# Opening's sums of squares moved into the loop over x, and the first two blocks of four down stages interleaved

## The chip, the cores and the metric

One core of one Trainium2 chip runs the whole program. The metric is the device time of one execution in microseconds (us), and a shorter time is better. Each kernel is executed several times; the median is given. A profile of one further execution gives the times of single instructions.

## The reference

A two-layer trunk works on 512 prompt tokens and 8 x 16 sample tokens, 640 columns in all, with a residual stream `x` of width 1024. Each layer does

```python
x = x + 0.5 * swiglu(rmsnorm(x, norm_g[i, 0]), ffn_w_gu[i, 0], ffn_w_d[i, 0])
x = x + mixer_i(rmsnorm(x, norm_g[i, 1]))      # even: gated DeltaNet and mLSTM heads; odd: gated short convolution
x = x + 0.5 * swiglu(rmsnorm(x, norm_g[i, 2]), ffn_w_gu[i, 1], ffn_w_d[i, 1])
x = x + (p[i] @ w_ple[i]) * sigmoid(rmsnorm(x, norm_g[i, 3]) @ w_ple_gate[i])

def rmsnorm(x, g):
    return x * rsqrt(mean(x * x) + EPS) * g
def swiglu(x, w_gu, w_d):
    a, b = split(x @ w_gu, 2)
    return (silu(a) * b) @ w_d
```

and a last rmsnorm follows. Everything is fp32. The hidden width of a feed-forward block is 2816.

## The kernel before

**Layout.** The residual stream lies transposed in SBUF: `x[:, q, :]` holds features 128q to 128q+127 on the partitions and all 640 tokens along the row, for q = 0 to 7. Every product is made of three matmuls per tile: high parts (`xh`, `hh`, `whi`) and low parts (`xl`, `hl`, `wlo`) of both operands, without the product of the low parts. A weight block of `kt` tiles of 128 x 128 times 640 tokens takes 6 matmuls of 320 columns per tile (`mm`, L898): high x high (L913) and high x low (L914) for both halves of the tokens, then low x high (L917). So a block of 8 tiles is 48 matmuls, and one of 6 tiles 36.

**The engines.** PE (TensorE) multiplies. SP issues the weight loads into `raw`, which has four places. ACT (ScalarE) casts a block of raw weights to `whi` (`prep(n)`, L1595, cast in L1607), POOL (GpSimd) subtracts to get `wlo` (L861), and DVE (VectorE) does most of what comes out of PSUM. `whi` and `wlo` are a ring of three places for blocks: `prep(n)` waits until the block that last had that place is done on PE. Each engine runs its own instruction list strictly in order, written out by hand; semaphores join them. `job_done` counts finished PE jobs; `lo_ready` counts finished `wlo`; `h_ready` counts finished hidden tiles; `xg_ready` counts finished tiles of the normed stream's low part; `slot_free` guards the four PSUM slots.

**The opening.** PE transposes x tile by tile (L982), and between these it runs step q of the first two weight blocks g0 and g0+1 (gate and up of the first hidden tile). Per tile, ACT copies x out of PSUM (L1787) and scales it to `xh` (L1650); DVE copies the sample columns (`x_rest`, L2723) and makes `xl` (`x_low`, L2269). DVE also has sums of x tiles to make for a fast form of the paired products that comes later, `tau_row`: for each of four i one `tau_back` (L2235) and four operations (`tau_sums`, L2228 to L2231), of which i = 0, 1, 2 lie in the loop. After the loop DVE copies three states out of PSUM (L2754 to L2756). Only then come the eight squares on ACT (L1813, alternately into `qcopy` and `stt`) and the eight additions on DVE (`square_sum`, L2278 and L2280, into `sumsq`), in lock step. PE runs block g0+2 meanwhile; then `norm_job` (L972, matmul in L968) needs the finished `sumsq`. Its root (ACT, L1732) and the reciprocal `r` (DVE, L2366) are needed by the gates. `plain_start` on DVE (called in the first feed-forward stage) does `tau_rest` 0 and 1 (the low part `tau_lo`, L2244), the reciprocal, the copied gate (L2822), `tau_sums_alone(3)`, the copied hidden tile, the gate of block 2, and so on down to the first pair's `wlo` (`pair_low`, L2197). Then come the paired products (L928 to L930). The first pair needs `pair_low(0, 0)` at its start and, 24 matmuls later, `pair_low(0, 1)` and all of `tau_lo`.

**The down stages.** Each of the four feed-forward blocks has its 22 hidden tiles in three parts, of 8, 8 and 6 tiles. After each part a down stage of eight blocks n0 to n0+7 follows, with kt = 8, 8 and 6. In it PE waits at each k of block n0 for hidden tile k. DVE does for block o: `ut = ps * r` (L2181), `x = ut * -0.5 + x` (L2919), and in the third part, the last, `produce`: the square's sum and `x_low` (L2280, L2269). ACT does for block o: `prep(n0+o+2)`, and in the last part the square (L1659) and `xh` (L1650) as soon as x is new. In the second feed-forward block of a layer the input p is transposed (`pT`, two jobs) behind block n0+1, and DVE copies and splits it (L2941, L2943) behind block n0+1's own work. What follows the four last parts is the even mixer's input projection, the first ple stage, the odd mixer's input projection and the second ple stage. The first block of each needs `xl` of all eight tiles.

These four last down stages are called A, B, C and D below, in order of time. The place in the ring that block n0+2 or n0+3 gets depends on how many blocks follow until the next pairs: in A and C, n0+2 has a place of its own and n0+3 takes the place of n0+1; in B, n0+2 takes the place of n0; in D, n0+3 takes that of n0.

## Time and profile before

| what | us |
|---|---|
| median of three runs | 2714.54 (2713.57 to 2715.55) |
| the profiled execution's own time | 2713.01 |
| its span, first to last instruction | 2711.3 |
| PE busy in it | 2652.8 (98%) |
| DVE busy | 1863.9 (69%) |
| ACT busy | 1075.4 (40%) |
| POOL busy | 524.6 (19%) |
| PE waiting for the sum of squares (L968) | 5.1 |
| PE waiting for hidden tiles' low parts (L2793) | 4.0 + 2.9 |

The mean granted TensorE clock of the execution is 0.991 of full speed. All times in the trace count from the first instruction. Timeline rows read: start, duration, engine, line, operation, output<-inputs, shapes, count, and in brackets the idle time ahead of it with what ended it. Matmul durations overlap, so the time of a piece of work on PE is read from start to start.

### The profile page before, as it was taken

How to read it: one execution, taken by the hardware profiler on the slowest of the kernel's cores; microseconds unless marked ns; L12 is line 12 of the kernel's file. 1: busy time of each engine (PE TensorE's matmuls, PEld its weight loads, DVE VectorE, ACT ScalarE, POOL GpSimd, SP SyncE). 2: the span in 40 equal slices, each digit the busy share in tenths (PEclk: the TensorE clock that was granted, in tenths of full speed). 3: DMA queues.
4: the chain of work that ended last, by engine and by line, in shares of the span. 5: the costliest groups of instructions: out<-in, count | busy, mean ns of one | idle time of the engine just before them, and what ended most of it. 6: DMA issues, size and time to landing. Idle time of an engine off the chain costs nothing.

```text
span 2711.3 us, 43605 instructions
## 1 busy us (share of the span) xinstructions
PE 2652.8 (98%) x18155; PEld 2613.9 (96%) x18155; DVE 1863.9 (69%) x2188; ACT 1075.4 (40%) x1565; POOL 524.6 (19%) x249
## 2 busy tenths in 40 slices
PE   7999999999999999999999999999999999999998
PEld 7999999999998799999999999999999999999998
DVE  7748386988667768576577874847666786584756
ACT  5525254233222645344244552524411254252545
POOL 1030303232010030201113302030333311102041
PEclk9999999999999999999999999999999999999999
DMA  4323223232003122323232232232222223232231
GB/s 122 86 71 89 83 75 90 55 81 55 17 9 86 54 72 78 94 78 94 63 88 70 71 101 71 78 94 75 83 78 79 63 78 94 63 95 65 82 101 50
DMA packets 401180, 205.57 MB, mean 76 GB/s; under 512 B 15586, under 2 KB 398971, under 8 KB 400984
## 3 DMA queue, kind: packets, MB, share of 16 engines
q1 hardware_dynamic: 400778, 202.70, 26.4%
q8 instruction: 144, 2.36, 0.4%
q14 instruction: 52, 0.43, 0.1%
q10 hardware_dynamic: 206, 0.08, 0.0%
HBM read 195.14 MB, written 7.60 MB: 75 GB/s over the span
## 4 chain that ended last, share of the span: by engine, by line
PE 54%; DVE 9%; ACT 2%; issue 1%; POOL 0%; DVEq 0%; ACTq 0%
PE ps L928 9%; PE ps L930 9%; PE ps L929 9%; PE ps L913 9%; PE ps L917 8%; PE ps L914 8%; DVE ut L2181 1%; DVE x L2919 1%; DVE sumsq L2280 1%; DVE r L2366 1%; DVE hf L2787 1%; DVE x L3105 0%; DVE wlo L2197 0%; DVE hl L2269 0%; PE ps L1198 0%
## 5 line engine op out<-in xcount | busy, mean ns | idle before, releaser
L861 POOL TENSOR_TENSOR wlo<-raw,whi 128x1024 fp32r<-128x1024 f32 (+2 forms) x212 | 513.1, 2423 | 2147.0 <-ACT whi L1607 2146.6
L913 PE MATMUL ps<-xh,whi 128*128 128x320 f32 x1520 | 464.0, 313 | 12.1 <-POOL wlo L861 4.7
L914 PE MATMUL ps<-xl,whi 128*128 128x320 f32 x1520 | 458.4, 309 | 0.0
L913 PE MATMUL ps<-hh,whi 128*128 128x320 f32 x1440 | 437.6, 312 | 5.1 <-DVE hl L2793 2.9
L914 PE MATMUL ps<-hl,whi 128*128 128x320 f32 x1440 | 434.8, 310 | 0.0
L928 PE MATMUL ps<-tau_hi,whi 128*128 128x320 f32 x1296 | 401.3, 310 | 2.1 <-DVE wlo L2197 2.0
L929 PE MATMUL ps<-tau_lo,whi 128*128 128x320 f32 x1296 | 400.5, 309 | 0.0
L930 PE MATMUL ps<-tau_hi,wlo 128*128 128x320 f32 x1296 | 400.5, 309 | 0.0
L1607 ACT CAST whi<-raw 128x1024 fp32r<-128x1024 f32 (+2 forms) x214 | 206.7, 967 | 395.0 <-PE ps L917 355.6
L917 PE MATMUL ps<-xh,wlo 128*128 128x320 f32 x1520 | 347.1, 310 | 0.0
L917 PE MATMUL ps<-hh,wlo 128*128 128x320 f32 x1440 | 329.1, 310 | 0.0
L2181 DVE TENSOR_TENSOR ut<-ps,r 128x640 f32<-128x640 f32 x112 | 92.4, 825 | 328.0 <-PE ps L917 327.0
L913 PEld LDWEIGHTS ps<-xh,whi 128*128 128x128 f32 x1520 | 286.3, 188 | 18.5 <-issue 11.0
L914 PEld LDWEIGHTS ps<-xl,whi 128*128 128x128 f32 x1520 | 286.3, 188 | 0.9 <-issue 0.2
L1618 ACT CAST whi<-raw 128x512 fp32r<-128x512 f32 (+1 forms) x243 | 185.0, 766 | 246.9 <-PE ps L930 125.6
L913 PEld LDWEIGHTS ps<-hh,whi 128*128 128x128 f32 x1440 | 271.4, 189 | 8.1 <-DVE hl L2793 4.5
L914 PEld LDWEIGHTS ps<-hl,whi 128*128 128x128 f32 x1440 | 271.3, 188 | 0.4
L917 PEld LDWEIGHTS ps<-xh,wlo 128*128 128x128 f32 x1520 | 254.7, 188 | 0.0
L928 PEld LDWEIGHTS ps<-tau_hi,whi 128*128 128x128 f32 x1296 | 243.2, 188 | 4.5 <-issue 3.9
L929 PEld LDWEIGHTS ps<-tau_lo,whi 128*128 128x128 f32 x1296 | 243.3, 188 | 0.0
L930 PEld LDWEIGHTS ps<-tau_hi,wlo 128*128 128x128 f32 x1296 | 243.3, 188 | 0.0
L917 PEld LDWEIGHTS ps<-hh,wlo 128*128 128x128 f32 x1440 | 241.4, 188 | 0.0
(433 smaller groups left out, 4829.4 us busy)
## 6 DMA issues: line engine op xcount, KB each, us to landing
raw<-in_ffn_w_gu SPq DMA_DIRECT2D x324, 256.0 KB, 3.9
raw<-in_ffn_w_d SPq DMA_DIRECT2D x64, 512.0 KB, 4.0
raw<-in_w_in_even SPq DMA_DIRECT2D x32, 512.0 KB, 4.1
raw<-in_ffn_w_d SPq DMA_DIRECT2D x32, 384.0 KB, 3.6
raw<-in_w_in_odd SPq DMA_DIRECT2D x24, 512.0 KB, 3.7
raw<-in_w_ple_gate SPq DMA_DIRECT2D x16, 512.0 KB, 3.9
raw<-in_ffn_w_gu SPq DMA_DIRECT2D x14, 512.0 KB, 4.6
raw<-in_w_out_even SPq DMA_DIRECT2D x8, 512.0 KB, 4.0
```

Of the source, the lines that this page charges most:

```text
L861: pool.tensor_tensor(ring(wlo, n), raw[:, slot, 0:kt, :], ring(whi, n).bitcast(fp32), ALU.subtract).then_inc(lo_ready, 1)
L913: pe.matmul(ps[j % 4][:, c, 0:HT], wh[:, k], hi[:, k, cs], start=(k == 0), stop=False)
L914: pe.matmul(ps[j % 4][:, c, 0:HT], wh[:, k], lo[:, k, cs], start=False, stop=False)
L917: last = pe.matmul(ps[j % 4][:, c, 0:HT], wl[:, k], hi[:, k, cs], start=False, stop=(k == kt - 1))
L928: pe.matmul(out, whi[:, w], hi(i), start=(start and i == 0), stop=False, skip_group_check=True)
L929: pe.matmul(out, whi[:, w], lo(i), start=False, stop=False, skip_group_check=True)
L930: last = pe.matmul(out, wlo[:, w], hi(i), start=False, stop=(i == KH - 1), skip_group_check=True)
L1607: act.copy(ring(whi, n), raw[:, raw_pos["block", n], 0:kt, :]).then_inc(hi_ready, 1)
L1618: act.copy(group_ring(whi, g), group_raw(p, g)).then_inc(pair_hi, 1)
L2181: o1(dve.tensor_tensor(out, a, b, ALU.mult))
L2280: own(dve.tensor_tensor(sumsq[:], sumsq[:], src, ALU.add).then_inc(sm, 1), sm)
L2366: o1(dve.reciprocal(r[:], r[:]))
```

## The change

On PE, in down stages with fewer than 8 tiles per block (the four last parts), the first two blocks run together: five k steps of n0, five of n0+1, then the sixth of n0 and the sixth of n0+1. Blocks n0+2 to n0+7 stay as they were.

On ACT, the square of tile q-2 stands inside the loop over x, behind `xh` of tile q, for q = 2 to 7; the squares of tiles 6 and 7 stand behind the loop, ahead of the copies of g0 and g0+1 and of `prep(3)`.

On DVE, the addition of tile q-3 stands inside the loop from q = 3, with `tau_back(0)` at q = 5. The tau sums 0, 1 and 2 leave the loop and stand behind the last addition, ahead of the reciprocal. In `plain_start`, `tau_rest(t, 1)` moves behind the copied gate and `tau_sums_alone(3)` behind the gate of block 2.

```diff
@@ PE
                 elif kind == "down":
                     if s.get("split"):
                         first_blocks(s)
+                    hidden = (h_ready, s["hbase"])
+                    both = s["kt"] < KD
+                    if both:
+                        for part in ((0, s["kt"] - 1), (s["kt"] - 1, s["kt"])):
+                            for o in range(2):
+                                mm(s["n0"] + o, *s["hid"], first=hidden, part=part)
                     for o in range(2 if s.get("split") else 0, KD):
-                        mm(s["n0"] + o, *s["hid"], first=(h_ready, s["hbase"]) if o == 0 else None)
+                        if not both or o > 1:
+                            mm(s["n0"] + o, *s["hid"], first=hidden if o == 0 else None)
@@ ACT
+                    def square(q):
+                        if q >= 2:
+
+                            act.wait_ge(sq_added, q - 1)
+                        act.activation([qcopy, stt][q % 2][:], x[:, q, :], ACT.Square).then_inc(sq_ready, 1)
+
                     for q, j in enumerate(s["x"]):
...
                         x_high(0, q, 0)
                         if q == 0:
                             prep(1)
+                        if q >= 2:
+                            square(q - 2)
                     prep(2)
...
-                    for q in range(KD):
-                        if q >= 2:
-
-                            act.wait_ge(sq_added, q - 1)
-                        act.activation([qcopy, stt][q % 2][:], x[:, q, :], ACT.Square).then_inc(sq_ready, 1)
-                        if q == 3:
-                            first_out(0, gt)
-                            prep(3)
-                        if q == 5:
-                            first_out(1, ut)
+                    square(KD - 2)
+                    square(KD - 1)
+                    first_out(0, gt)
+                    prep(3)
+                    first_out(1, ut)
@@ DVE
                         x_low(0, q, 0)
-                        i = q // 2 - 1
-                        if i >= 0 and q % 2 == 0:
-                            tau_back(i)
-                        elif i >= 0:
-                            tau_sums(0, i, 0)
+                        if q >= 3:
+                            square_sum(0, q - 3)
+                            dve.sem_inc(sq_added, 1)
+                        if q == 5:
+                            tau_back(0)
...
-                    for q in range(KD):
+                    for q in range(KD - 3, KD):
                         square_sum(0, q)
                         dve.sem_inc(sq_added, 1)
+                    tau_sums(0, 0, 0)
+                    tau_sums_alone(1)
+                    tau_sums_alone(2)
@@ DVE, plain_start
                         tau_rest(t, 0)
-                        tau_rest(t, 1)
                         norm_recip(s)
                         copied_gate()
-                        tau_sums_alone(3)
+                        tau_rest(t, 1)
                         copied_hidden()
                         plain_gate(1)
+                        tau_sums_alone(3)
                         tau_rest(t, 2)
```

On PE at the start of down stage A, before: n0 accumulates in `ps3`, n0+1 in `ps0`. The first row is the end of step k = 4 of n0, the next five are its last step.

```order
2523 L917 MATMUL ps3<-hh_56,wlo_54 128x320 x2
2524 L913 MATMUL ps3<-hh_56,whi_53 128x320 [waits h_ready]
2525 L914 MATMUL ps3<-hl_57,whi_53 128x320
2526 L913 MATMUL ps3<-hh_56,whi_53 128x320
2527 L914 MATMUL ps3<-hl_57,whi_53 128x320
2528 L917 MATMUL ps3<-hh_56,wlo_54 128x320 x2
2529 L913 MATMUL ps0<-hh_56,whi_53 128x320 [waits lo_ready,slot_free0]
```

The same rows of the changed kernel:

```order
2523 L917 MATMUL ps3<-hh_56,wlo_54 128x320 x2
2524 L913 MATMUL ps0<-hh_56,whi_53 128x320 [waits h_ready,lo_ready,slot_free0]
2525 L914 MATMUL ps0<-hl_57,whi_53 128x320
2526 L913 MATMUL ps0<-hh_56,whi_53 128x320
2527 L914 MATMUL ps0<-hl_57,whi_53 128x320
2528 L917 MATMUL ps0<-hh_56,wlo_54 128x320 x2
2529 L913 MATMUL ps0<-hh_56,whi_53 128x320 [waits h_ready]
```

The last step of n0 now stands 30 matmuls later, behind five steps of n0+1, and n0 and n0+1 end within six matmuls of each other. The same happens in stages B, C and D.

On DVE in the opening, before: from the last addition of the squares to the copied hidden tile.

```order
47 L2280 TENSOR_TENSOR sumsq<-sumsq,stt 128x640 [waits dve_own,sq_ready]
48 L2244 TENSOR_TENSOR tau_lo<-tau_row,tau_hi 128x1280 [waits sumsq_done,tau_high]
49 L2244 TENSOR_TENSOR tau_lo<-tau_row,tau_hi 128x1280 [waits tau_high,tau_low]
50 L2366 RECIPROCAL r<-r 128x640 [waits root_ready,tau_low]
51 L2822 TENSOR_TENSOR gt<-gt,r 128x640 [waits slot_free2,dve_own]
52 L2235 TENSOR_SCALAR xg_back<-x,vec_109 128x320 [waits gate_in]
```

The same stretch of the changed kernel:

```order
33 L2290 TENSOR_TENSOR sumsq<-sumsq,stt 128x640 [waits dve_own,sq_ready]
34 L2238 SCALAR_TENSOR_TENSOR tau_row<-x,vec_109,xg_back 128x320 [waits sumsq_done,back_ready]
35 L2239 SCALAR_TENSOR_TENSOR tau_row<-x,vec_109,xg_back 128x320 [waits dve_own]
...
47 L2241 SCALAR_TENSOR_TENSOR tau_row<-x,vneg,tau_row 128x320 [waits dve_own]
48 L2254 TENSOR_TENSOR tau_lo<-tau_row,tau_hi 128x1280 [waits tau_high,tau_ready]
49 L2376 RECIPROCAL r<-r 128x640 [waits root_ready,tau_low]
50 L2835 TENSOR_TENSOR gt<-gt,r 128x640 [waits slot_free2,dve_own]
51 L2254 TENSOR_TENSOR tau_lo<-tau_row,tau_hi 128x1280 [waits tau_high,gate_in]
```

The last addition moves from place 47 to place 33 of DVE's list, but the reciprocal only from 50 to 49: fourteen tau operations stand between them now, and one `tau_lo` moved behind the gate. DVE's list up to the first pair holds the same instructions in both.

## Rows read from the trace of the kernel before

**Rows 1.** Waits of PE: engine, line waited for: us in total, times, longest.

```profile
PE ps L968 <- DVE sumsq L2280: 5.1, 2, 4.9
PE ps L913 <- DVE xl L2793: 4.0, 6, 1.5
PE ps L913 <- DVE hl L2793: 2.9, 6, 0.8
```

**Rows 2.** Timeline of PE, opening: g0+2's last matmuls, the norm's, first tau product.

```profile
40.77 0.46 PE L917 MATMUL ps<-xh,wlo 128*128 128x320 f32 x2
46.09 2.50 PE L968 MATMUL ps<-sumsq,one 128*128 128x320 f32 x4 [4.87 <-DVE sumsq L2280]
...
74.10 0.31 PE L928 MATMUL ps<-tau_hi,whi 128*128 128x320 f32 x1
```

**Rows 3.** Busy time by stretches: us, PE, PEld, DVE, ACT, POOL (x), PEclk, DMA share, GB/s.

```profile
46.09:50.80 4.71, 4.71 (x14) 3.92 (x15) 3.39 (x3) 4.51 (x5) 2.54 (x1) 0.50 0.32 88
1416.45:1448.20 31.75, 31.75 (x219) 31.75 (x218) 24.76 (x31) 11.53 (x17) 11.13 (x6) 1.00 0.17 50
```

**Rows 4.** Timeline of DVE, opening.

```profile
30.14 2.61 DVE L2228 SCALAR_TENSOR_TENSOR tau_row<-x,vec,xg_back 128x320 f32<-128x320 f32 x1
32.78 0.55 DVE L2229 SCALAR_TENSOR_TENSOR tau_row<-x,vec,xg_back 128x320 f32<-128x320 f32 x1
...
40.66 2.46 DVE L2280 TENSOR_TENSOR sumsq<-sumsq,qcopy 128x640 f32<-128x640 f32 x1 [1.09 <-ACT qcopy L1813]
46.19 3.02 DVE L2244 TENSOR_TENSOR tau_lo<-tau_row,tau_hi 128x1280 fp32r<-128x1280 f32 x2
50.40 4.15 DVE L2366 RECIPROCAL r<-r 128x640 f32<-128x640 f32 x1 [1.19 <-ACT r L1732]
...
66.86 1.22 DVE L2197 TENSOR_TENSOR wlo<-raw,whi 128x1024 fp32r<-128x1024 f32 x1
...
70.42 1.76 DVE L2197 TENSOR_TENSOR wlo<-wsum,whi 128x1536 fp32r<-128x1536 f32 x1
```

**Rows 5.** Timeline of POOL, opening: the low part of block g0+2.

```profile
30.02 2.37 POOL L861 TENSOR_TENSOR wlo<-raw,whi 128x1024 fp32r<-128x1024 f32 x1 [25.35 <-ACT whi L1607]
```

**Rows 6.** Timelines of DVE, ACT, POOL and PE, down stage A and its end.

```profile
427.05 0.83 DVE L2919 SCALAR_TENSOR_TENSOR x<-ut,x 128x640 f32<-128x640 f32 x1
...
432.33 2.46 DVE L2919 SCALAR_TENSOR_TENSOR x<-ut,x 128x640 f32<-128x640 f32 x1
...
467.80 0.89 DVE L2269 SCALAR_TENSOR_TENSOR xl<-x,vec,xh 128x640 fp32r<-128x640 f32 x1
...
431.35 0.84 ACT L1607 CAST whi<-raw 128x768 fp32r<-128x768 f32 x1 [1.97 <-PE ps L917]
...
432.26 1.85 POOL L861 TENSOR_TENSOR wlo<-raw,whi 128x768 fp32r<-128x768 f32 x1 [5.77 <-ACT whi L1607]
...
468.93 0.31 PE L913 MATMUL ps<-xh,whi 128*128 128x320 f32 x1
```

**Rows 7.** Timelines of ACT, DVE, POOL and PE, down stage B and the ple stage's start.

```profile
1410.42 0.84 ACT L1607 CAST whi<-raw 128x768 fp32r<-128x768 f32 x1 [2.22 <-PE ps L917]
...
1411.40 2.47 DVE L2919 SCALAR_TENSOR_TENSOR x<-ut,x 128x640 f32<-128x640 f32 x1
...
1411.33 1.86 POOL L861 TENSOR_TENSOR wlo<-raw,whi 128x768 fp32r<-128x768 f32 x1 [7.76 <-ACT whi L1607]
...
1429.92 2.05 POOL L861 TENSOR_TENSOR wlo<-raw,whi 128x768 fp32r<-128x768 f32 x1 [6.84 <-ACT whi L1607]
...
1432.38 0.31 PE L913 MATMUL ps<-hh,whi 128*128 128x320 f32 x1
...
1452.82 0.38 PE L913 MATMUL ps<-xh,whi 128*128 128x320 f32 x1 [0.32 <-issue]
```

**Rows 8.** Timelines of POOL and PE, down stage D and the second ple stage's start.

```profile
2600.64 2.06 POOL L861 TENSOR_TENSOR wlo<-raw,whi 128x768 fp32r<-128x768 f32 x1 [6.84 <-ACT whi L1607]
...
2636.37 0.38 PE L913 MATMUL ps<-hh,whi 128*128 128x320 f32 x1 [0.99 <-issue]
```

## The prediction, made before the changed kernel was run

> **What bounds the kernel now.** I read three views: PE's waits, for where it loses time; the timelines of all engines around those waits, for what a removed wait runs into; and the busy time by stretches, for the clock and for PE's pace. PE is busy for nearly the whole span, so an edit can win only a wait on PE or a stretch of low clock, and lose only by a new one. Two waits are aimed at. One is for the sum of squares, 4.87 us at once: the last matmul of block g0+2 begins at 40.92, the norm's at 46.09 [rows 1, 2]. Behind it PE works until 50.80 at a granted clock of 0.50, so at 1.2 GHz, and 0.50 x 4.71 = 2.4 us of work are lost with it [rows 3]. The other is for the low part of the sixth hidden tile in down stages A to D: 0.84 us each in A to C, where the wait for `hl` is at most 0.8, and 1.5 in D [rows 1]; with the pipeline's restart about 1.0, 1.0, 1.0 and 1.7, 4.7 us in all. PE's pace at full clock: the six blocks n0+2 to n0+7 of stage B take 31.75 us [rows 3], 5.29 a block of 36 matmuls, 0.88 a k step, 0.147 a matmul.
>
> **The rule that decides both parts.** When a DVE operation with both inputs in SBUF starts while POOL subtracts, it ends after POOL does: the tau sum at 30.14 took 2.61 us and ended at 32.75, POOL ran from 30.02 to 32.39; its next neighbour takes 0.55 [rows 4, 5]. The new x of n0+1 in stage A began at 432.33, took 2.46 instead of 0.83 and ended at 434.79, 0.68 after POOL's 434.11 [rows 6]. Operations that read PSUM aren't held up.
>
> **Part 1, down stages.** Five steps of n0+1 are put ahead of n0's last: 30 x 0.147 = 4.4 us. The hidden tile is late by 1.0 (D: 1.7), so this wait on PE goes whole. But n0 now ends at 66 matmuls from the stage's start instead of 36 and the wait: 9.69 instead of 6.39, so 3.3 us later (D: 2.6). On n0's end hangs a chain: DVE's `ut` and new x, ACT's square and `xh`, ACT's cast of a later block (in order behind them), POOL's `wlo`, DVE's next new x, held until POOL ends, and round again. One round is 0.03 + 1.37 on ACT, 0.90 for the cast, 2.04 on POOL, 0.68 on DVE: 5.0 us, and 5.6 for blocks of 8 tiles. PE needs 5.29. So the chain runs nearly at PE's pace and a delay at its head isn't made good in six rounds; its two ends are the next blocks' `wlo` and the eighth `xl`.
> Stage B. The cast of n0+2 waits for n0's end (ring place), at 1410.42; then POOL from 1411.33 to 1413.19 and the new x until 1413.87 [rows 7]. All of it moves 3.3 later. POOL ends block n0+2 at 1416.5, where PE would want it at 1415.4: 1.2 us of waiting, which eats the 1.0 won. Three blocks on, `wlo` of n0+5 ended at 1431.97 and PE began that block at about 1432.3, so 0.35 us of slack [rows 7]; with 3.3 it ends at 1435.3, and PE, whose own time for it would be 1432.5, waits 2.7 us. The ple stage's first gate began right behind a wait for POOL, at 1452.82 [rows 7]: no slack, so it moves the full 3.3. Stage B: +3.3 us.
> Stage A. n0+2 has a place of its own. The cast of n0+3 waited for n0+1's end and began at 431.35 [rows 6]. n0's new x ends at 427.88 + 3.3 = 431.18; with 1.40 for square and `xh` the cast begins at 432.58, 1.23 later, and so do POOL and every round behind. PE at n0+3: POOL ends at 435.35, PE wants it at 435.28, a wait of 0.2. The eighth `xl` ended at 468.69 and PE began with it at 468.93, 0.24 of slack [rows 6]; now 469.92, and with 0.1 for the restart PE is 1.1 later than before: a new wait of 1.9 us replaces one of 1.0. What follows is a DVE and ACT chain from the norm on and moves with it. Stage A: +1.1. Stage C has the same ring places and the same rows 1494.9 us later, with the same slack: +1.1.
> Stage D. n0 ends 2.6 later; n0+1's new x, which POOL didn't hold up before, now meets POOL and gets 2.2 later, and the chain with it. `wlo` of n0+5 ended at 2602.70 [rows 8], now 2604.9, PE wants it at 2602.5: a wait of 2.4. Then the ple stage's eight short blocks go through ACT's casts and copies, and the first gate waits behind POOL at 2636.37 [rows 8]. +2.1, and at least +0.8 if that piece has slack that I don't see.
> Sum: 3.3 + 1.1 + 1.1 + 2.1 = +7.6 us. Bounds: if none of the chain's delay reaches PE, -4.7; if all chains move by 3.3, +13. I take 7.6, since in each stage the row at the end has a slack of 0.35 us or less.
> The Trainium skill, "Perfetto Trace Analysis", Optimization Strategy, says to work on what blocks the matmul engine when it idles; by that alone the four waits go and the part is worth -4.7 us. No run here shows that yet, and the rows above speak against it.
>
> **Part 2, the opening.** The squares and additions of tiles 0 to 4 fill DVE's time in the loop where tau sums stood. A walk with the rows' durations: PE's two short waits for `xl` in the loop (1.05 together with restarts) go, g0+2 ends at 39.7, `sumsq` is done at 35.4, so PE doesn't wait for it, and the norm ends at 40.5. Then g0+3 to g0+5 take 3 x 7.05 and PE wants the first pair at 61.7, where before it began near 70.6. That would be 8.9 us.
> But DVE must have done the same list first. From the first addition until `wlo` at 70.42 ends (72.18), DVE before has two waits, 1.09 and 1.19, and two holds by POOL, 2.06 and 1.63 [rows 4]. Now: sum done 35.4; tau sums 0 to 2, 7.9 us, of which the second operation meets POOL's block g0+3 (35.8 to 38.3) and loses 2.0: 45.4; ACT's cast of g0+4 comes behind the high part of tau 1, so POOL runs from 45.0 to 47.6 and holds the first `tau_lo`: 49.0 instead of 47.0. The root is ready by 47.1. The reciprocal starts at 49.0, 1.4 earlier than its 50.40 [rows 4]. Behind it stands all that stood there, 21.8 us until the end at 72.18, and one `tau_lo` of 1.5 more (two take 3.02) [rows 4]: 72.3. The first pair's `wlo` (66.86 + 1.2 [rows 4]) comes at 68.1 as before. So PE waits 6.2 us ahead of the first pair instead of 4.9 ahead of the norm. Its third product, at 74.10 [rows 2], can start at 72.3 at full clock: 1.8 won. After a wait of this length the clock was low until 4.7 us behind the restart [rows 3]; then the two first products take 5.9 instead of 3.5 us and it starts at 74.1: nothing won. I take -0.7, between these; -1.8 and +0.9 (low clock for longer) are the bounds.
> Who meets POOL first decides 2 us of this. The Trainium skill, "SBUF — State Buffer", Who interferes with whom, says that whoever issues first gets the shared port pair for the whole instruction. By it, if the cast of g0+4 comes a few tenths later, `tau_lo` is first and the reciprocal starts at 47.1: 1.9 us more won here. The trace agrees with the rule: in rows 4 and 5 POOL is first and DVE waits.
> The rest (the copies of g0 and g0+1 and `prep(3)`, 3 to 4 us earlier on ACT; the raw loads of the first pair, which wait for POOL) has cover of several us and costs nothing.
>
> **Sum.** 7.6 - 0.7 = +6.9 us. The profiled execution took 2713.01 us, 1.53 under the median; 2719.9 there, 2721.4 against the median of 2714.54.
>
> **Rivals.**
> 1. The chain has slack that I don't see, as meant by the edit: the down stages win 4.7 and the opening 0.7: 2709.1. For it: DVE is busy only 69% and has waits in every round. Against: the waits are for ACT and POOL in the same chain.
> 2. The opening gives its 8.9 us, since DVE or POOL are quicker there than I walked, and the down stages cost 7.6: 2713.2. It needs DVE to save 7 us in a list that is the same.
> 3. Both: 2714.5 - 8.9 - 4.7 = 2700.9, faster.
> 4. The new waits, 6.2 us in the opening, 2.7 in B, 2.4 in D, each bring a stretch of low clock. Each costs up to 1.7 us; in B and D part of it lies in the slack of the rounds behind. Slower: 2723 to 2726, say 2724.5. It counts from the point where a wait of 2.4 to 2.7 us is followed by clock 0.50; the wait of 1.5 in D [rows 1] wasn't.
>
> **How the numbers follow.** My forecast, 2721.4 with 2718.5 to 2724, gets 0.62; rival 1 0.10, rival 2 0.12, rival 3 0.04, rival 4 0.12. The range from 2712.5 to 2725.5 leaves out rivals 1 and 3 and the tail of 4, 0.18. A difference under 0.2%, 5.4 us, can't be told from none here. Slower by more is above 2720.0: 0.62 less 0.08 for its lower end, and 0.12 of rival 4: 0.66. Within: 0.08, rival 2 and half of rival 1: 0.25. Faster by more: 0.09.
>
> **What would show it.** In the profile after: PE no longer waits at L968; it waits some 6 us for DVE's `wlo` ahead of L928 near 62 us, and pair 0's tau products begin near 73. In stages A to D no wait for L2793; instead `wlo` (L861) waits of 1.2 and 2.7 us in B and of 2.4 in D, and `xl` (L2269) waits of 1.9 at the first block behind A and C. New x of n0 3.3 us later against the stage's start, of n0+7 1.2 (A, C), 3.3 (B), 2.2 (D). It is wrong if the last new x isn't later, or if DVE reaches the reciprocal before 46.

## The result, and the profile after

| | before | after |
|---|---|---|
| median of 20 runs each, us | 2713.35 (2707.69 to 2721.57) | 2722.64 (2716.47 to 2730.21) |
| profiled execution, us | 2713.01 | 2728.32 |
| its span, us | 2711.3 | 2726.6 |
| ratio | | 1.0036 [1.0025, 1.0046] |

The changed kernel is slower: +9.8 us by the ratio (6.8 to 12.5), +9.3 by the medians. The prediction had +6.9 and 2721.4.

PE's waits in the changed kernel (engine, line waited for: us in total, times, longest), against [rows 1]:

```profile
PE ps L913 <- POOL wlo L861: 11.7, 16, 2.7
...
PE ps L928 <- DVE wlo L2207: 6.6, 10, 3.7
PE ps L913 <- DVE xl L2279: 3.7, 2, 2.1
PE ps L913 <- DVEq L2195: 2.9, 1, 2.9
...
PE ps L913 <- DVE hl L2279: 1.7, 1, 1.7
...
PE ps L913 <- DVE hl L2806: 1.3, 4, 0.3
```

The wait of 4.9 us for `sumsq` is gone, and of the waits for `hl` and `xl` of the hidden tiles (now L2806) only eight of at most 0.3 us are left. In their place stand waits for POOL's `wlo`, up to 2.7 us, for the eighth `xl` ahead of the next stage, 1.67 behind A and 1.68 behind C (in the row with `hl` of L2279, since the low parts of the next stage's operand lie in that buffer there), and in the opening 2.9 for a slot of PSUM and 3.7 for the first pair's `wlo`. The 2.1 us in the row for `xl` of L2279 is no new wait: it lies at 12.60 us, in the loop over x, where the kernel before waits 2.35.

**Opening.** Timelines of PE, DVE and POOL in the changed kernel:

```profile
39.66 0.70 PE L968 MATMUL ps<-sumsq,one 128*128 128x320 f32 x2
...
57.90 0.41 PE L913 MATMUL ps<-xh,whi 128*128 128x320 f32 x1 [2.86 <-DVEq L2195]
...
68.89 0.61 PE L928 MATMUL ps<-xh,whi 128*128 128x320 f32 x1 [3.69 <-DVE wlo L2207]
...
35.60 2.68 DVE L2238 SCALAR_TENSOR_TENSOR tau_row<-x,vec,xg_back 128x320 f32<-128x320 f32 x1 [0.57 <-DVE sumsq L2290]
...
45.18 2.79 DVE L2241 SCALAR_TENSOR_TENSOR tau_row<-x,vneg,tau_row 128x320 f32<-128x320 f32 x1
48.00 1.49 DVE L2254 TENSOR_TENSOR tau_lo<-tau_row,tau_hi 128x1280 fp32r<-128x1280 f32 x1
49.52 4.15 DVE L2376 RECIPROCAL r<-r 128x640 f32<-128x640 f32 x1
...
35.52 2.41 POOL L861 TENSOR_TENSOR wlo<-raw,whi 128x1024 fp32r<-128x1024 f32 x1 [3.11 <-ACT whi L1614]
45.21 2.41 POOL L861 TENSOR_TENSOR wlo<-raw,whi 128x1024 fp32r<-128x1024 f32 x1 [7.28 <-ACT whi L1614]
48.54 3.22 POOL L861 TENSOR_TENSOR wlo<-raw,whi 128x1024 fp32r<-128x1024 f32 x1 [0.92 <-ACT whi L1614]
```

PE reaches the norm 6.4 us earlier (46.09 before [rows 2]) and doesn't wait for it. But the reciprocal starts at 49.52, where it started at 50.40 [rows 4], since POOL holds two DVE operations ahead of it, 2.68 and 2.79 us where the neighbours take 0.55. PE then waits 2.9 and 3.7 us.

**Stage B.** Timelines of ACT, POOL, DVE and PE in the changed kernel, the answers to [rows 7]. This stage begins 7.60 us later than in the kernel before (ACT's `hh` of the sixth hidden tile, 1407.47 and 1415.07), so 7.60 is to be taken off:

```profile
1421.31 0.84 ACT L1614 CAST whi<-raw 128x768 fp32r<-128x768 f32 x1 [5.51 <-PE ps L917]
...
1422.23 1.80 POOL L861 TENSOR_TENSOR wlo<-raw,whi 128x768 fp32r<-128x768 f32 x1 [11.06 <-ACT whi L1614]
1422.29 2.42 DVE L2932 SCALAR_TENSOR_TENSOR x<-ut,x 128x640 f32<-128x640 f32 x1
...
1424.18 0.38 PE L913 MATMUL ps<-hh,whi 128*128 128x320 f32 x1 [0.99 <-POOL wlo L861]
...
1440.78 2.00 POOL L861 TENSOR_TENSOR wlo<-raw,whi 128x768 fp32r<-128x768 f32 x1 [6.84 <-ACT whi L1614]
...
1442.92 0.60 PE L913 MATMUL ps<-hh,whi 128*128 128x320 f32 x1 [2.67 <-POOL wlo L861]
...
1460.54 1.05 ACT L1614 CAST whi<-raw 128x1024 fp32r<-128x1024 f32 x1 [0.83 <-PE ps L917]
...
1461.67 2.96 POOL L861 TENSOR_TENSOR wlo<-raw,whi 128x1024 fp32r<-128x1024 f32 x1 [0.53 <-ACT whi L1614]
```

The cast of n0+2 comes 3.29 us later against the stage (1413.71 for 1410.42), n0's new x ends 3.24 later, POOL's low part of n0+5 ends at 1435.18 instead of 1431.97, 3.21 later: the whole delay is still there after three rounds. PE waits 1.0 and 2.7 us for it. Behind the second wait the clock is low (0.52, so mostly at 1.2 GHz); busy time of that stretch, with the granted clock as the third last number:

```profile
1442.92:1446.32 3.40, 3.40 (x13) 3.40 (x14) 2.46 (x4) 2.18 (x3) 0.58 (x1) 0.52 0.13 39
```

The ple block's cast, which waits for PE, comes 4.1 us later (1448.84 before), its low part on POOL ends 4.3 later, and so does the first gate: 1464.73 for 1452.82 [rows 7], less 7.60: +4.31.

**Stages A and D.** DVE and PE behind stage A; PE in stage D:

```profile
469.76 0.89 DVE L2279 SCALAR_TENSOR_TENSOR xl<-x,vec,xh 128x640 fp32r<-128x640 f32 x1
...
470.70 0.42 PE L913 MATMUL ps<-xh,whi 128*128 128x320 f32 x1 [1.67 <-DVE xl L2279]
...
2618.20 0.39 PE L913 MATMUL ps<-xh,whi 128*128 128x320 f32 x1 [2.30 <-POOL wlo L861]
```

The eighth `xl` ends 0.05 us before PE takes it, as the slack of 0.24 in [rows 6] let expect, and PE waits 1.67 us there. In D the wait for n0+5 is 2.3 us.

### The profile page after: what moved, and what is told of

Same layout as the page of the kernel before. It is cut to its first block, busy times and chain, and to the rows that moved or that the text cites. A ratio compares the mean times of both kernels' runs of the same rounds, so it can differ in the third digit from the quotient of the medians.

```text
span 2726.6 us, 43607 instructions
## 1 busy us (share of the span) xinstructions
PE 2661.7 (98%) x18155; PEld 2621.2 (96%) x18155; DVE 1862.6 (68%) x2188; ACT 1074.2 (39%) x1565; POOL 524.8 (19%) x249
## 4 chain that ended last, share of the span: by engine, by line
PE 80%; DVE 16%; ACT 2%; issue 1%; POOL 0%; DMA 0%; DVEq 0%; SPq 0%; ACTq 0%
PE ps L928 12%; PE ps L930 12%; PE ps L929 12%; PE ps L913 11%; PE ps L917 11%; PE ps L914 11%; PE ps L1057 3%; DVE x L2932 2%; PE ps L1083 2%; DVE ut L2191 1%; DVE sumsq L2290 1%; DVE ct L2987 1%; DVE r L2376 1%; DVE ct L2984 1%; PE ps L1051 1%
```

## The experiments

**How they are read.** The medians move by whole steps from one execution to the next: the same changed kernel took 2716 to 2730 us. So each kernel's profile is also cut into stretches that are compared one by one, from a fixed matmul to a fixed matmul: A from the last pair's first tau product ahead of the stage to the norm behind it (before: 385.98 to 469.81), B 1333.30 to 1459.93, and C, D and what lies between 1530.12 to 2643.48. The stretch from 469.81 to 1033.68 stands apart. Differences to the kernel before, in us; the last two columns are the length of that stretch, and where PE starts pair 0's tau products (74.10 before):

| kernel | A | B | C to D | 469.81 to 1033.68 | tau products |
|---|---|---|---|---|---|
| before | 0 | 0 | 0 | 563.87 | 74.10 |
| changed | +1.17 | +4.32 | +3.43 | 569.60 | 74.79 |
| changed, once more | +1.13 | +4.35 | +3.38 | 568.69 | 73.58 |
| down stages alone | +1.18 | +4.36 | +3.26 | 562.70 | 74.17 |
| stage B alone | 0.0 | +4.36 | 0.0 | 563.92 | 74.59 |
| opening alone | 0.0 | 0.0 | +0.12 | 565.54 | 74.46 |
| opening, fewer additions | 0.0 | 0.0 | -0.06 | 562.09 | 72.73 |
| one step ahead | -0.88 | -0.06 | -1.38 | 569.29 | 74.55 |
| one step, once more | -0.89 | -0.06 | -1.35 | 566.11 | 74.70 |
| three steps ahead | -0.57 | +1.44 | -0.19 | 569.29 | 74.83 |
| root first | 0.0 | 0.0 | +0.16 | 559.87 | 72.68 |
| root first, tau low part late | 0.0 | 0.0 | +0.15 | 563.18 | 70.60 |
| root first, one step | -0.89 | -0.03 | -1.19 | 563.80 | 72.03 |
| all three | -0.88 | -0.04 | -1.16 | 571.04 | 69.93 |

**The down stages alone** (e_down), and **the opening alone** (e_open): the two halves of the change, one each. The diff shows the first; the second is the change without it.

```diff
-for o in range(2 if s.get("split") else 0, KD):
-    mm(s["n0"] + o, *s["hid"], first=(h_ready, s["hbase"]) if o == 0 else None)
+hidden = (h_ready, s["hbase"])
+both = s["kt"] < KD
+if both:
+    for part in ((0, s["kt"] - 1), (s["kt"] - 1, s["kt"])):
+        for o in range(2):
+            mm(s["n0"] + o, *s["hid"], first=hidden, part=part)
...
```

> The kernel before with the interleaved first two blocks in the four last down stages, opening as before. Theory (delay at the head of a chain of DVE, ACT and POOL): the stretches of the trace from n0's start to the next stage move by +1.2, +4.3, +1.2 and +2.1 us as in the profile after, +8.8 in all, and the time is 1.0030 to 1.0035 of before; no wait for the hidden tile's low part is left in the four stages. Rival (the cost sits elsewhere: in the profile after, the mixer's core between 656 and 1038 us took 5.8 us more than before): then the core is 5 to 6 us longer here as well, and the four stages together cost under 5.

Measured: 2720.29 us, ratio 1.0035 [1.0024, 1.0046].

> The kernel before with the new order in the opening alone. Theory (DVE's list up to the first pair is the floor): no wait at the norm, but waits of about 3 us at block g0+5 and 3.7 us ahead of the first pair; the down stage that began at 138.8 in before's trace begins 0.7 later; the time is within 0.1% of before. Rival (the opening wins once the down stages don't hide it): 4 to 9 us faster, 0.997 to 0.9985. The core between the first projection and the second feed-forward block takes what it took before, within what single profiles scatter.

Measured: 2713.36 us, ratio 0.9991 [0.9976, 1.0005]. So the down stages carry all of the loss, 8.8 us by the stretches, and the opening nothing that a median shows. Pair 0's tau products begin between 74.10 and 74.83 us in six profiles with the old opening and between 73.58 and 74.79 in three with the new one; the means are 0.2 us apart. Most of the spread within one kernel is the clock: in the changed kernel PE starts the first pair at 68.89 and the 5.90 us until the tau products go at a granted clock of 0.57, in its second profile it starts at 69.36 and needs 4.22 us at 1.00. There the low clock came earlier, behind the wait of 2.85 us for the slot (0.54 over the 3.40 us from 58.37), and it only shortened the wait ahead of the first pair, 2.16 us instead of 3.69. The stretch from the first pair to the tau products, in the first profile and in the second:

```profile
68.89:74.79 5.90, 5.90 (x25) 5.90 (x26) 5.58 (x7) 2.71 (x5) 0.00 (x0) 0.57 0.00 0
...
69.36:73.58 4.22, 3.76 (x24) 3.50 (x24) 4.04 (x5) 2.75 (x6) 0.00 (x0) 1.00 0.00 0
```

**Stage B alone** (e_down_b).

```diff
-both = s["kt"] < KD
+both = s["kt"] < KD and "pT" in s and s["layer"] == 0
```

> Interleaved only in the down stage ahead of the first ple stage (B). Theory: B's stretch is 3.3 to 4.3 us longer (4.3 if the wait of 2.7 us ahead of block n0+5 brings a stretch of low clock, 3.3 if not), all other stages as before. Rival (the four stages' costs depend on each other, or the low clock alone makes B's cost): B costs under 2 us by itself.

Measured: 2717.42 us in one run. Stage B costs the same 4.36 us with the others undone, so its cost doesn't come from them.

**One step ahead instead of five** (e_one_step), **three** (e_three_steps). The last step of n0 waits for the sixth hidden tile; one or three steps of n0+1 are put ahead of it (the diff is the one with one step; with three, 3 stands for both 1s of n + 1).

```diff
...
+mm(n, *s["hid"], first=hidden, part=(0, kt - 1))
+mm(n + 1, *s["hid"], first=hidden, part=(0, 1))
+mm(n, *s["hid"], first=hidden, part=(kt - 1, kt))
+mm(n + 1, *s["hid"], part=(1, kt))
...
```

> Down stages A to D with one k step of n0+1 (6 matmuls, 0.88 us) ahead of n0's last instead of all five; opening as in the kernel before. Theory (a chain through ACT's cast, POOL and DVE starts at n0's end and has almost no slack): the step fills 0.88 of the wait of about 1.0 for the hidden tile, and n0 ends 0.1 to 0.2 us EARLIER than before, so no chain is late. Stages A and C win 0.9 each, since there the ring place is n0+1's, whose end moves 0.9 forward too; B, whose ring place is n0's, wins 0.1 to 0.5; D 0 to 0.9, since its hidden tile is 1.7 late. Sum -2 to -3 us, ratio 0.9990 to 0.9993, and no wait for wlo over 1 us. Rival (any step of n0+1 ahead of n0 brings the cost, by the ring places or by two blocks that end close together): +1 us or more, with wlo waits of 2 us in B and D as in the changed kernel.

Measured: 2716.21 us, ratio 1.0011 [1.0002, 1.0020], on its face the rival's result. By the stretches the down stages do what the theory says, A -0.88, B -0.06, C -0.87 and D -0.45, -2.3 in all; PE's wait for n0+5 in B is 0.45 us at 1437.06, and only one wait for `wlo` in D, 1.17 us at 2629.86, is above the 1 us that the theory allowed. The loss lies elsewhere (569.29 us for 563.87 in this profile), in the stretch behind 469 us that has none of these stages in it; it comes back below.

> As the last, with three k steps of n0+1 ahead (18 matmuls, 2.64 us). n0 ends 1.6 us later than before in A to C, 0.9 in D. Theory, with a threshold in each stage: A and C: the cast of n0+3 is bound by n0's new x only from 2.07 us of delay on, so nothing of the loss and the whole gain, -1.0 each; B: the chain moves the full 1.6 less its slack of 0.35, +1.3, and its wait for wlo of n0+5 shrinks from 2.7 to about 1.3 with no low clock behind it; D +0.4. Sum -0.3 us. Rival (the cost grows evenly with the steps put ahead, between one and five): +3.4 us.

Measured: 2719.12 us, ratio 1.0016 [1.0004, 1.0027]; stretches A -0.57, B +1.44, C -0.58, D +0.41, in all +0.7, where the theory had -0.3 and a cost that grows evenly +3.4. In A and C the cost doesn't grow evenly: against the one step, a delay of n0 of 1.6 us costs 0.3 there, and one of 3.3 costs 2.1. A line through the two begins at a delay of about 1.3 us, an estimate; the 2.07 that was expected is too high. In B 1.6 us of delay cost 1.5. The wait for n0+5 in B is 2.2 us, not 1.3 as written: PE comes 0.9 earlier and POOL 1.6 later, and the text had only counted the second. The clock stays at 1.00 behind it:

```profile
1439.17:1442.57 3.40, 3.40 (x23) 3.40 (x24) 2.46 (x4) 2.18 (x3) 0.57 (x1) 1.00 0.13 39
```

**What DVE has to do ahead of the reciprocal** (e_few_sums): the opening alone, with the additions of tiles 1 to 6 to the sum of squares left out (the sum then holds two of eight tiles, and the time is that of a kernel which does less).

```diff
+def few_sum(q):
+    if q in (0, KD - 1):
+        square_sum(0, q)
+    else:
+        dve.wait_ge(sq_ready, q + 1)
+    dve.sem_inc(sq_added, 1)
```

> The new order in the opening alone, with the additions of the squares of tiles 1 to 6 left out (the waits and signals around them stay), so the opening's norm is computed from two tiles of eight. It takes some 5 us of DVE work away ahead of the reciprocal. Theory (DVE's list is the floor): the reciprocal starts 3 to 5 us earlier than the 49.5 of the changed kernel, and the first pair's tau products 3 to 6 us earlier than 74.8. Rival (PE's, ACT's or POOL's own chain or the PSUM slot of block g0+5 is the floor): under 1.5 us.

Measured: 2709.75 us in one run. Counted from the transposes of the conv state (30.68 in the opening alone, 29.56 here, since the two executions are 1.1 us apart by then), the reciprocal starts at 18.67 instead of 20.19, 1.5 us earlier, and the first pair at 38.04 instead of 39.55, 1.5 earlier. That is half of the 3 us that the theory had at least, and at the rival's bound of 1.5. Four of the six additions lie inside the loop and two behind it, and two additions of 0.83 us are about what was won; that the four lie in DVE's spare time is concluded from this and not measured by itself. PE's start of the first pair moves with the reciprocal, one for one, so no other engine's chain is the floor within these 1.5 us.

**Who is first, POOL or DVE** (e_root_first): opening alone, with the norm's root on ACT ahead of the cast of g0+4, so that POOL starts later.

```diff
 tau_round(s["tau"], 1)
-prep(g0 + 4)
 norm_root(s)
+prep(g0 + 4)
```

> The opening of the changed kernel alone, down stages as before, with one exchange on ACT: the norm's root ahead of the cast of block g0+4. Theory (who starts first, POOL or a DVE operation with both inputs in SBUF, decides about 2.2 us): POOL's low part of g0+4 starts 2 us later, the last operation of the third tau sum takes 0.55 instead of 2.79 and the reciprocal starts 2.2 us earlier than in the opening alone (50.87 there, norm at 41.00). All of DVE's list up to the first pair moves with it as it did by 2.6 us where additions were left out: first pair's wlo at about 66.7, pair 0's tau products at about 72.5 instead of 74.46, ratio 0.9985. Rival: POOL meets another DVE operation there (the first tau_lo) and holds it as long: no change against the opening alone, 0.9991.

Measured: 2707.73 us, ratio 0.9982 [0.9970, 0.9993]. Timelines of DVE, POOL and PE:

```profile
46.32 0.55 DVE L2234 SCALAR_TENSOR_TENSOR tau_row<-x,vneg,tau_row 128x320 f32<-128x320 f32 x1
46.91 1.49 DVE L2247 TENSOR_TENSOR tau_lo<-tau_row,tau_hi 128x1280 fp32r<-128x1280 f32 x1
48.43 4.15 DVE L2369 RECIPROCAL r<-r 128x640 f32<-128x640 f32 x1
52.62 1.49 DVE L2828 TENSOR_TENSOR gt<-gt,r 128x640 f32<-128x640 f32 x1
...
48.73 4.69 POOL L861 TENSOR_TENSOR wlo<-raw,whi 128x1024 fp32r<-128x1024 f32 x2 [9.66 <-ACT whi L1607]
...
51.23 0.38 PE L913 MATMUL ps<-xh,whi 128*128 128x320 f32 x1 [2.16 <-POOL wlo L861]
...
68.45 0.38 PE L928 MATMUL ps<-xh,whi 128*128 128x320 f32 x1 [1.36 <-DVE wlo L2200]
```

The held operation, 2.79 us at 45.18 in the changed kernel, takes 0.55, and the reciprocal starts 2.2 us earlier, counted as above (17.96 for 20.19). POOL now holds the gate's product instead, 1.49 us where it takes 0.82, so 1.6 us reach the first pair. PE waits 2.16 for POOL at 51.23, and the clock is at 0.69 over the 3.40 us behind it, which costs nothing: both are given back in the shorter waits later, none for the slot of PSUM and 1.36 us ahead of the first pair, instead of 2.86 and 2.15. Nothing but the order of two pieces of work on ACT was changed.

**A shorter list ahead of the first pair** (e_tau_late): the last of the above, and `tau_rest(t, 3)`, the last low part of the taus, behind both low parts of the first pair.

```diff
 else:
-    tau_rest(t, 3)
     plain_hidden(1)
...
 pair_low(p0, 1)
+if s["plain"] <= 3:
+    tau_rest(t, 3)
```

> Opening with the root ahead of the cast, down stages as before, and in addition DVE's last low part of the taus (1.48 us) behind the low parts of the first pair instead of ahead of them. Theory (PE's first pair waits for nothing but DVE's list, so what is taken out of the list ahead of it comes off the time in full): the first pair begins 1.5 us earlier than in the opening with the root ahead alone (68.46 there), pair 0's tau products at about 71.2 instead of 72.68; the moved low part ends at about 72.4, when PE wants it at 72.5. Ratio 0.9977, some 2706.5. Rival (the first pair is bound by ACT or by the transfers of its weights too): less than 0.5 us earlier.

Measured: 2708.82 us, ratio 0.9980 [0.9965, 0.9995]. DVE and PE:

```profile
68.57 1.76 DVE L2200 TENSOR_TENSOR wlo<-wsum,whi 128x1536 fp32r<-128x1536 f32 x1
70.24 1.49 DVE L2247 TENSOR_TENSOR tau_lo<-tau_row,tau_hi 128x1280 fp32r<-128x1280 f32 x1
...
70.60 0.42 PE L928 MATMUL ps<-tau_hi,whi 128*128 128x320 f32 x1 [0.47 <-ACT sq L1828]
```

The tau products begin at 40.70 counted from the same transposes, 42.21 with the root first alone: 1.5 us earlier, the whole 1.48 of the moved operation. The median doesn't show it; the stretch behind 469 us took 3.3 us more in this profile.

**One step and root first** (e_best), **all three** (e_all_three).

> One step ahead in the down stages and the opening of the changed kernel with the root ahead of the cast of g0+4, together. By the theory the two sums add: -2.5 and -4 us, about 2707, ratio 0.9976. By the rivals of both: +1 and -2, about 2712.5, ratio 0.9996.

Measured: 2709.47 us, ratio 0.9992 [0.9980, 1.0004]. The interval leaves out the theory's 0.9976 and holds the rival's 0.9996. Outside the stretch behind 469 us the profile is 4.1 us shorter than that of the kernel before, where the two sums had 6.5.

> The same opening with one step ahead in the down stages. By the theory, outside the stretch in which the clock differs from execution to execution, -2.3 us from the down stages and -2.9 from the opening against the kernel before, 5.2 in all; the median carries what that stretch adds or takes (-4 to +5.7 us): 2708 if it is as in most runs of before, range 2703.5 to 2713.5. Rival: the one step ahead makes that stretch longer for good (+5.4): 2713.

Measured: 2710.11 us, ratio 0.9986 [0.9972, 0.9999]. Outside the stretch behind 469 us the profile of all three is 6.2 us shorter than that of the kernel before (2135.1 us for 2141.3, up to the last matmul), in it 7.2 us longer. Root first, root first with the late low part, and all three have intervals below 1; among these three the runs tell no winner. What the edits themselves are shown to win is less clear-cut than the medians: outside the stretch root first is 1.2 us shorter than before and with the late low part 3.6, each in one profile, while the median of root first is 5.5 us below that of before in the same batch (2713.27, 35 runs). Some 4.3 us of its win lie in the stretch.

**Chance or kernel** (e_after_again, e_one_step_again): the changed kernel and the one with one step, unchanged, executed and profiled once more.

> The changed kernel once more, unchanged, for one look. Outside the stretch from the norm of layer 0's first half to the second layer's first pair (469.8 to 1033.7 us in the kernel before, 563.9 us long) every stretch should last as in the first profile of it, within 0.3 us. In that stretch the profiles so far took 559.9 to 569.6 us, with the same instructions and different places of low clock. Theory: this is chance of the execution, so the stretch may take another of these times (563.9 or less) here, with everything else alike. Rival: each kernel has its own time there, set by its order, and the changed one takes 569.6 again.

Measured: 2726.19 us; the stretch took 568.69 us, 569.60 in the first profile, everything else as in the table.

> The kernel with one step ahead once more, unchanged, for one look. In its first profile the down stages were 0.9, 0.05, 0.9 and 0.45 us shorter than before (-2.3, as expected), and the stretch from 469 to 1039 us took 569.3 instead of 563.9 us. Theory (chance of the execution): the down stages again -2.3 within 0.3, and that stretch anywhere from 559.9 to 569.6. Rival (the stretch is longer because of the edit): 569.3 again in both this and the changed kernel.

Measured: 2713.55 us; the stretch 566.11, after 569.29. Its row in the changed kernel's first and second profile, in that of one step ahead, first and second, and root first, in this order (the third last number is the granted clock):

```profile
471.70:1041.30 569.60, 551.62 (x3869) 523.92 (x3867) 436.29 (x583) 193.90 (x338) 98.38 (x41) 0.96 0.20 54
```

```profile
470.51:1039.20 568.69, 549.82 (x3870) 522.60 (x3868) 436.18 (x583) 193.82 (x338) 98.43 (x41) 0.96 0.21 54
```

```profile
469.37:1038.66 569.29, 550.03 (x3869) 522.41 (x3868) 436.38 (x583) 193.84 (x337) 98.09 (x41) 0.96 0.20 54
```

```profile
469.54:1035.65 566.11, 546.83 (x3869) 520.43 (x3867) 436.28 (x583) 193.53 (x338) 98.10 (x41) 0.97 0.21 54
```

```profile
468.54:1028.41 559.87, 541.00 (x3869) 514.97 (x3867) 436.26 (x583) 193.76 (x337) 98.35 (x41) 0.98 0.21 55
```

DVE, ACT and POOL are busy for the same time within 0.4 us in all five; what differs is PE's time and the granted clock. The clock that is lost in the stretch (its length times one minus the granted clock) is 10.2 us with the root first, 15.4 before, 22.2 in the changed kernel and 23.9 in all three, and in all fourteen profiles the length follows it within 1.4 us. All but 0.3 us of the difference arises between 378 and 530 us from the stretch's start. 30 us of it, in the kernel before, in the changed one and with the root first:

```profile
879.81:909.81 30.00, 28.36 (x194) 26.74 (x194) 21.42 (x39) 20.86 (x39) 0.00 (x0) 0.83 0.04 11
```

```profile
881.70:911.70 30.00, 28.42 (x167) 26.75 (x167) 18.93 (x35) 19.29 (x37) 0.00 (x0) 0.69 0.04 11
```

```profile
878.54:908.54 30.00, 29.28 (x205) 27.85 (x205) 21.64 (x34) 23.19 (x47) 0.00 (x0) 0.83 0.03 10
```

The length of this stretch changes from one execution to another of the same kernel, by 3.2 us in one pair and 0.9 in the other, and the times of a kernel's runs lie in groups some 4 to 9 us apart (before near 2709, 2713 and 2722; changed near 2717, 2723 and 2728). So much is shown. That all kernels draw their time there from the same set with the same odds is not: both profiles of the changed kernel are at the long end, nine of ten runs with the root first lie within 1.3 us of 2707.1, and all seven with the down stages alone within 1.6 us of each other. For two kernels the intervals speak against it: what the profiles show outside the stretch would give a ratio of 0.9993 with one step ahead, below its interval from 1.0002, and 0.9996 with the root first, above its interval up to 0.9993. Their typical time in the stretch differs from that of before, by an estimate from the medians some 4.9 us more and 4.3 less. Why is not shown. The moment at which a kernel comes to the stretch gives no simple order: starts at 464.86, 468.54, 471.07 and 471.70 were followed by 571.04, 559.87, 562.70 and 569.60 us.

## Why the prediction was right, and where it wasn't

- **The sign and the main mechanism were right.** 2722.64 lies in the range, 1.2 us above the forecast, and slower by more than 0.2% had 0.66. The difference to before is 9.3 to 9.8 us instead of 6.9: the two medians of before, 1.2 us apart, hide part of the error, which is luck. The stretches and the opening together give +8.7; what is missing up to 9.3 or 9.8 is less than the stretch behind 469 us differs from one execution to the next.
- **Stage A +1.1 and C +1.1:** measured +1.13 to +1.18 in three profiles, with the new wait of 1.67 us for the eighth `xl` where the text had 1.9. Right. The one-step and three-step kernels show the reason: a delay of 1.6 us costs 0.3 there and one of 3.3 costs 2.1, so the first microsecond or so is made good.
- **Stage D +2.1:** measured +2.11 to +2.14 (C to D +3.26 to +3.43 in all, forecast 3.2), with a wait of 2.3 us for n0+5, forecast 2.4. Right.
- **Stage B +3.3:** measured +4.3 to +4.4. This is the term that was mis-sized. The chain moved by 3.2 as worked out, and the waits are 1.0 and 2.7 us where 1.2 and 2.7 were written. The extra 1.0 came in behind the second wait, where the clock was 0.52 over 3.40 us, which takes 1.6 us of work from PE; the ple block's cast, which waits for PE, then came 4.1 late instead of 3.2, and POOL with it. With three steps ahead the wait is 2.2 us, the clock stays at 1.00, and B costs 1.44 for a delay of 1.6. This is rival 4's mechanism, and here it cost 1.0; it had 0.12. Its price of up to 1.7 us a stretch, for which no row stood there, was about right for what PE loses: 1.6 here, 1.7 in the opening, where it shows in one profile of three. In D it cost nothing. That the low clock makes the extra 1.0 is read from the timeline and this comparison; no run took the low clock alone away.
- **In D the same mechanism cost nothing.** With the down stages alone the clock fell behind D's wait too, in the changed kernel it didn't, and D cost the same, +2.14 and +2.12: the slack of the rounds behind took it, as rival 4's text allowed. Later waits for `wlo` gave it back: 0.55 and 1.34 us in the changed kernel (2636.58 and 2641.68), one of 0.59 at the second place with the down stages alone (2634.04). Granted clock of the 3.4 us behind that wait, down stages alone and changed kernel:

```profile
2610.57:2613.97 3.40, 3.40 (x14) 3.40 (x15) 2.46 (x4) 2.18 (x3) 0.58 (x1) 0.54 0.14 39
```

```profile
2618.20:2621.60 3.40, 3.40 (x23) 3.40 (x24) 2.46 (x4) 2.18 (x3) 0.57 (x1) 1.00 0.13 39
```

- **Opening -0.7:** measured -0.2 by the means, within what executions differ. The frame was right: PE goes on behind the norm at 40.5, as written, the wait returns ahead of the first pair, and DVE's list decides. The step that failed is the reciprocal's start, "49.0 instead of 50.40": it began at 49.52, 50.00 and 50.87 in the three profiles. The spread is older than the reciprocal: counted from the transposes of the conv state it starts at 20.19 in all three, and at 19.6 in all six profiles with the old opening, so by this count it comes 0.6 us later and not earlier. What the new opening wins lies ahead of these transposes, 1.0 us in the mean. Both holds by POOL came as written, the second on the last tau sum rather than on `tau_lo`, but they took 2.13 and 2.24 us where 2.0 were allowed, and the first tau sum waited 0.57 more. Missed altogether was PE's wait of 2.9 us for a slot of PSUM at 57.90, which `plain_gate(1)` frees. PE is there at 55.0, 8.5 us earlier than before, and that gate on DVE starts at 56.96, only 2.2 us earlier; the wait only takes its part of the one that follows. The two are 6.5 us together; the text had 6.2, though its own 68.1 and 61.7 give 6.4.
- **The sentence on who meets POOL first** was borne out: moved by one exchange on ACT, the reciprocal came 2.2 us earlier (the text had 1.9), and the kernel is faster than before (ratio 0.9982), though most of that lies in the stretch behind 469 us.
- **The rule to work on what blocks PE** (the Trainium skill, "Perfetto Trace Analysis", Optimization Strategy) gave -4.7 us for the down stages. All the waits it points at did go, and the part cost 8.8: the rows were right against it. Where only as much work was moved as the wait was long, the four stages won 2.3.
- **Rival 1** (the chain has slack) is true of A and C for about the first microsecond of delay, and false of the 3.3 us that the change brings. **Rivals 2 and 3** didn't come: the list on DVE is the same and takes the same time.

## What to carry to other kernels

When PE waits for the last tile of an operand, put just as much other work ahead of that step as the wait is long: here one step of 0.88 us for a wait of 1.0 won 2.3 us in the four stages (the kernel as a whole came out 0.1% slower, as the stretch behind 469 us was longer), and five steps lost 8.8, because what hangs on the first block's end came 3.3 us late. Before moving work, follow the loop that starts at the delayed output (here ACT's cast, POOL, DVE) once round: if a round takes about as long as PE's own block, a delay at its head is still there at the stage's end. And when an engine's list decides, look for the neighbour that holds it; exchanging two pieces of work on a third engine brought the tau products 1.6 us forward, the whole rebuild of the opening 0.2. And compare by stretches, with the clock beside them, before calling a median's few microseconds a win or a loss.

## What the runs showed of the hardware

- At a granted clock near 0.5 PE does 13 or 14 matmuls in 3.40 us, at 1.00 it does 23. The same wait of 2.3 us in stage D was followed by low clock in one execution (down stages alone) and by none in two (the changed kernel); behind the one of 2.7 in B there was some in all four profiles that have it. A wait of 2.2 us was followed by none in B with three steps and ahead of the first pair (opening alone, changed kernel once more), but by some in all four kernels with the root first, at 50 to 51 us (0.51 to 0.71 over the 3.40 us behind it). So the length of the wait alone doesn't tell. In the opening the stretch from the first pair to the tau products took 5.90 us once and 4.22 us once, with the same instructions.
- The stretch from 469.81 to 1033.68 took between 559.9 and 571.0 us over fourteen profiles of twelve kernels, with the other engines' busy times the same. A difference of 5 us between two profiles or two medians of this kernel can be this alone; the other stretches repeated within 0.1 us from a kernel's first profile to its second, apart from the opening.
- POOL's subtraction holds a DVE operation with both inputs in SBUF, 2.68 and 2.79 us for 0.55, and the hold goes the other way too: POOL's block at 48.54 began 0.54 us behind DVE's `tau_lo` and took 3.22 us instead of 2.41. With the reciprocal, which reads one tile, neither waited: it took 4.15 us with POOL beside it for nearly all of that time, and POOL needed 4.69 for two blocks. That is how the Trainium skill, "SBUF — State Buffer", Who interferes with whom, has it: DVE with one input in SBUF (outside its 2-port modes) does not contend, with two it does, and whoever issues first keeps the ports for the whole instruction. The rows agree on all three points.
